# Expert weights read with eight neighbouring rows per partition, in a mixture-of-experts inference step

## What is computed

```python
logits = t @ w_router + b_router                # 320 x 32
top_v, top_i = lax.top_k(logits, 4)             # four experts per token
gates = jax.nn.softmax(top_v, axis=-1)
# for each expert, on the tokens that chose it:
uu  = xb @ w_up[eid] + b_up[eid]                # (n,1024) @ (1024,2048)
glu = jnp.minimum(uu[:, :1024], 7.0)
lin = jnp.clip(uu[:, 1024:], -7.0, 7.0)
act = glu * jax.nn.sigmoid(1.702 * glu) * (lin + 1.0)
yb  = act @ w_down[eid] + b_down[eid]           # (n,1024) @ (1024,1024)
```

## Time and profile before

| | |
|---|---|
| runs | 1298.5, 1301.34, 1304.66 us; median 1301.34 us |
| profiled execution, first to last instruction | 1299.7 us |
| TensorE busy | 1211.8 us, 93% |
| VectorE, ScalarE, GpSimd busy | 28%, 20%, 3% |
| read from HBM | 438 MB, 340 GB/s over the span |
| first up product to the end | 306.3 us to 1299.7 us |

### The profile page before, as it was taken

The page is one execution under the profiler, slowest core; times in us unless marked ns, Lnnn a source line. Parts: engine busy times, 40 slices in busy tenths (PEclk is TensorE's granted clock), DMA queues, the critical chain, the costliest instruction groups (busy, mean ns, idle before and its releaser), DMA issues.

```text
span 1299.7 us, 14599 instructions
## 1 busy us (share of the span) xinstructions
PE 1211.8 (93%) x5802; PEld 579.9 (45%) x5802; DVE 361.8 (28%) x668; ACT 259.9 (20%) x415; POOL 36.5 (3%) x90
## 2 busy tenths in 40 slices
PE   5999999998999999999999999999999999999995
PEld 4788789893333333333333333333333333333331
DVE  3545675622112222121212121222122121212123
ACT  5463352412111111111111111111111111111112
POOL 2002400000000000000000000000000000000000
PEclk9999999998889999999999999999999999999998
DMA  8550524479889999999999999999999999999861
GB/s 296 214 198 1 178 85 146 165 286 403 345 351 377 418 413 417 413 417 412 412 419 413 420 412 419 413 417 413 418 413 418 412 417 416 412 420 371 344 255 42
DMA packets 90801, 442.27 MB, mean 340 GB/s; under 512 B 3915, under 2 KB 16787, under 8 KB 57968
## 3 DMA queue, kind: packets, MB, share of 16 engines
q1 hardware_dynamic: 57952, 312.75, 59.8%
q10 hardware_dynamic: 31760, 125.85, 24.3%
q0 software_dynamic: 1056, 3.21, 0.7%
HBM read 438.06 MB, written 3.73 MB: 340 GB/s over the span
## 4 chain that ended last, share of the span: by engine, by line
PE 89%; DVE 4%; ACT 4%; issue 2%; ACTq 1%; POOL 0%; DVEq 0%; POOLq 0%
PE ps L441 35%; PE ps L455 17%; PE ps L331 14%; PE ps L462 7%; PE ps L418 7%; ACT regionP L588 2%; DVE regionP L724 2%; PE ps L433 1%; DVE regionP L688 1%; PE ps L1702 1%; PE ps L424 1%; ACTq L611 1%; PE ps L430 1%; ACT regionP L624 1%; PE ps L1487 1%
## 5 line engine op out<-in xcount | busy, mean ns | idle before, releaser
L441 PE MATMUL ps<-regionA,regionP 128*64 128x512 f32 x1024 | 224.9, 597 | 14.0 <-DVE regionP L688 14.0
L441 PE MATMUL ps<-regionB,regionP 128*64 128x512 f32 x1024 | 226.1, 600 | 0.0
L455 PE MATMUL ps<-regionD,regionP 128*64 128x512 f32 x992 | 218.2, 592 | 0.0
L667 DVE TENSOR_TENSOR regionP<-ps,regionP 128x512 f32<-128x512 f32 x32 | 22.1, 692 | 673.4 <-PE ps L448 673.4
L441 PEld LDWEIGHTS ps<-regionA,regionP 128*64 128x64 f32 x1024 | 74.4, 138 | 155.5 <-issue 152.4
L441 PEld LDWEIGHTS ps<-regionB,regionP 128*64 128x64 f32 x1024 | 72.7, 138 | 139.5 <-issue 139.2
L455 PEld LDWEIGHTS ps<-regionD,regionP 128*64 128x64 f32 x992 | 72.2, 137 | 140.7 <-issue 140.4
L604 ACT ACTIVATE regionP<-ps 128x1024 f32<-128x1024 f32 x32 | 32.7, 1023 | 458.3 <-PE ps L441 458.3
L462 PE MATMUL ps<-regionP 128*128 128x512 f32 (+1 forms) x192 | 94.0, 613 | 19.4 <-DVE regionP L724 13.2
L418 PE MATMUL ps<-regionP 128*64 128x512 f32 x384 | 92.0, 615 | 7.1 <-ACT regionP L588 4.8
L331 PE MATMUL ps<-roundedP,roundedA 128*128 128x320 f32 x272 | 85.3, 313 | 1.3 <-DVE regionP L1335 1.3
(11 more groups left out here) (276 smaller groups left out, 1034.1 us busy)
## 6 DMA issues: line engine op xcount, KB each, us to landing
regionA<-in_w_up SPq DMA_DIRECT2D x64, 2048.0 KB, 13.2
regionB<-in_w_up SPq DMA_DIRECT2D x64, 2048.0 KB, 10.7
regionD<-in_w_down ACTq DMA_DIRECT2D x60, 2048.0 KB, 18.0
regionA<-in_w_in SPq DMA_DIRECT2D x4, 2048.0 KB, 13.9
regionB<-in_w_mk SPq DMA_DIRECT2D x4, 1024.0 KB, 9.7
regionD<-in_w_mv SPq DMA_DIRECT2D x4, 1024.0 KB, 22.7
regionD<-in_w_out SPq DMA_DIRECT2D x4, 1024.0 KB, 12.5
regionD<-in_w_mq SPq DMA_DIRECT2D x4, 1024.0 KB, 5.0
```

What stands on the lines that cost most here:

```text
L441: ins = pe.matmul(ps[64 * half:64 * half + 64, n_, :], XTe[:, k % 4, k // 4, :], w[:, k, 1024 * half + 512 * n_:1024 * half + 512 * n_ + 512],
L455: ins = pe.matmul(ps[64 * n_:64 * n_ + 64, 6, :], lin[:, k, :], w[:, k, 512 * n_:512 * n_ + 512], start=(k == 0), stop=(k == KT - 1))
L667: dve.tensor_tensor(glu, u[:, :, 0:SLOTS], be[:, 0:8].unsqueeze(2).broadcast_to([P, KT, SLOTS]), ALU.add).then_inc(S("glu"), 1)
```

## The change

The contraction rows are dealt to the partitions in another way: partition p holds the eight neighbouring rows 8p to 8p+7, and block k is made of the rows 8p + k. A load of 2 MB then reads, for each partition, one piece of 16 KB (two rows of 8 KB, or four of 4 KB) at a distance of 64 KB (`w_up`) or 32 KB (`w_down`) from that of the next partition. Whatever meets the weights in a product is permuted to match: the tokens' columns (`Hm`), the gain (`g_rows`, loaded a second time in the new order), the up bias (`rows_of`) and the columns of `U`. The three reads that do the permuting step over eight elements (32 bytes) from one element to the next.

```diff
+        g_rows = small[:, 144:152]
@@ up_src, down_src, and the first loads in the SyncE block
-            return src.rearrange("a (k p) f -> p (a k) f", p=P)
+            return src.rearrange("a (p k) f -> p (a k) f", p=P)
@@ moe_act
+            def turned_rows(act):
+                return act.activation(U.rearrange("s (k p) -> s k p", k=KT),
+                                      ps[:, 0:2, :].rearrange("s b f -> s (b f)").rearrange("s (p k) -> s k p", k=KT), ACT.Copy)
...
-                act.activation(U[:, :], ps[:, 0:2, :].rearrange("p b f -> p (b f)"), ACT.Copy).then_inc(S("up_read"), 1)
+                turned_rows(act).then_inc(S("up_read"), 1)
@@ moe_dve
-                g = g_moe.rearrange("p (h q) -> p q h", h=2).unsqueeze(3).broadcast_to([P, 4, 2, SLOTS])
+                g = g_rows.rearrange("p (h q) -> p q h", h=2).unsqueeze(3).broadcast_to([P, 4, 2, SLOTS])
...
+            dve.wait_ge(S("g_rows_in"), 16)
             tokens().then_inc(S("tokens_in"), 1)
@@ GpSimd block
             pool.dma_start(buprow[0:E, :], a["b_up"][0]).then_inc(S("bup_in"), 16)
+            pool.dma_start(g_rows, a["norm_moe"][0].rearrange("(p k) -> p k", k=KT)).then_inc(S("g_rows_in"), 16)
@@ ScalarE block
-                act.activation(Hm[0:n, i, :], acc[0:n, i, :], ACT.Copy, scale=rs2[0:n, i:i + 1]).then_inc(S("Hm"), 1)
+                act.activation(Hm[0:n, i, :].rearrange("t (k p) -> t k p", k=KT), acc[0:n, i, :].rearrange("t (p k) -> t k p", k=KT),
+                               ACT.Copy, scale=rs2[0:n, i:i + 1]).then_inc(S("Hm"), 1)
@@ TensorE block
-            turn("bup", [(E * f, buprow[0:E, 128 * f:128 * f + 128], E, P) for f in range(16)])
+            rows_of = buprow[0:E, :].rearrange("e (h p k) -> e h k p", h=2, k=KT)
+            turn("bup", [(E * f, rows_of[:, f // KT, f % KT, :], E, P) for f in range(16)])
```

More of the change, by code:

```diff
@@ L810, in load_up0 @@
             def load_up0(i):
-                load(upA[:, 2 * i:2 * i + 2, :], a["w_up"][0, 0].rearrange("(k p) f -> p k f", p=P)[:, 2 * i:2 * i + 2, :], f"upA_in{i}")
+                load(upA[:, 2 * i:2 * i + 2, :], a["w_up"][0, 0].rearrange("(p k) f -> p k f", p=P)[:, 2 * i:2 * i + 2, :], f"upA_in{i}")
             has(sp, "oT3")
@@ L824, in _ @@
             for i in range(4):
-                load(upB[:, 2 * i:2 * i + 2, :], a["w_up"][0, 1].rearrange("(k p) f -> p k f", p=P)[:, 2 * i:2 * i + 2, :], f"upB_in{i}")
+                load(upB[:, 2 * i:2 * i + 2, :], a["w_up"][0, 1].rearrange("(p k) f -> p k f", p=P)[:, 2 * i:2 * i + 2, :], f"upB_in{i}")
             has(sp, "mo7")
@@ L829, in _ @@
             for i in range(2):
-                load(wdn[:, 4 * i:4 * i + 4, :], a["w_down"][0, 0].rearrange("(k p) f -> p k f", p=P)[:, 4 * i:4 * i + 4, :], f"down_in{i}")
+                load(wdn[:, 4 * i:4 * i + 4, :], a["w_down"][0, 0].rearrange("(p k) f -> p k f", p=P)[:, 4 * i:4 * i + 4, :], f"down_in{i}")
             moe_sync(sp)
```

## The result

The changed kernel takes 1305.55 us, the median of 20 runs (1299.85 to 1309.99), where the kernel before takes 1299.4 us on the same chip (20 runs, 1295.32 to 1305.0). The ratio over all runs is 1.0044, with a 95% interval of 1.0027 to 1.0061: about 5.7 us slower (the medians lie 6.2 us apart), within the 0.5% that was called no change, and twice to three times the 2.2 us of the forecast. The profiled execution took 1304.0 us. First its page: span, busy time by engine, and the DMA strip.

What follows compares the result with a forecast made beforehand. TensorE's order of work was taken to set the time, the DMA right behind; loop gain 0, prologue costs 0.35 + 0.6 + 0.7 + 0.55 = 2.2 us on the 1301.34 us median gave 1303 us, 8-in-10 range 1296 to 1311.

Steps and rivals of the forecast that it cites:

- What bounds the kernel: Steady expert loop: TensorE's order of work sets the time, 60.61 us per pair, with the DMA right behind it.
- the thin margin: Expert loop: the second half of w_down lands only 0.9 us before TensorE's down product needs it.
- The 16 KB pieces: Weight loads: 623 ns per piece, DMA share from 101.5% to 98.6%; hidden behind TensorE, so gain costed at 0.
- Rival A: Expert loop: the DMA falls behind and TensorE waits for w_down in every expert, 1316 to 1329 us; chance 0.10.
- The decisive piece of 641 ns: Weight loads: above this time per 16 KB piece, the DMA would ask for more per expert than before.
- The copy of U: ScalarE's stepped copy after the up product: hidden except for the first expert, 0 to 0.7 us, taken as 0.35.
- Hm: Three stepped ScalarE copies ahead of the first gather: 0 to 2.2 us, taken as 1.1, half given back, 0.6.
- The bias's turn: 16 TensorE instructions in the prologue with a stepped stationary operand: 0 to 1.5 us, taken as 0.7.
- the load of g_rows: GpSimd's extra load issue ahead of the iota in the prologue, covered by nothing: 0.55 us, between 0.50 and 0.96.
- The sum: Prologue costs together: 0.35 + 0.6 + 0.7 + 0.55 = 2.2 us, between 0.5 and 5.4 us.
- Rival B: Prologue: stepped reads at their upper ends, 5.4 us, plus one more slow-clock stretch, 2.6 us: 1309 us; chance 0.08.
- First up product at 307 to 310: Sign that the forecast is right: the first up product starts at 307 to 310 us instead of 306.3.

Runs made afterwards that it cites:

- the layout alone: Changed kernel with new weight layout and copy of U kept, but bias, Hm and gain as before and no g_rows load: 1301.26 us, ratio 1.0006.
- the reads alone: Changed kernel with its permuted reads and g_rows load kept, but the weights laid out as before: 1306.23 us, ratio 1.0057 to the kernel before.
- second mended version: Changed kernel with Hm read with the step from PSUM and g_rows loaded behind the iota, bias still turned: 1299.61 us, ratio 1.0013.
- first mended version: Changed kernel with Hm read from PSUM, g_rows loaded behind the iota, bias loaded permuted in 32-byte pieces and not turned: 1305.02 us, ratio 1.0048.

## Why the prediction was right, and where its sum was off

**What bounds the kernel: right.** The pair stayed at 60.6 us, no product of the steady part waits for weights, and the layout alone is at 1.0006. Half the up work taken away gave nothing before, so the DMA did stand right behind TensorE, as the thin margin said.

**The 16 KB pieces: right, in price and in worth.** Forecast 623 ns and 98.6%; measured 623 and 615 ns, 98.4%. Costed at 0; the runs gave -0.2 us. What the step missed is a second reason why `w_down`'s margin grows: its pieces are now as large as those of `w_up`, so that, with turns by piece and work in both queues, it gets half of the bytes where it got a third. Rival A (the DMA falls behind) did not happen. The decisive piece of 641 ns was not reached: pieces 32 or 64 KB apart cost nothing to be seen. The 3% that the Trainium skill ("DMA: Bandwidth & Descriptors", "Latency and other measured facts") reports for rows 512 KiB apart do not show at these distances: the changed kernel with half the up blocks moved 428 GB/s over 500 us, where the steady part before had 415.

**The copy of U: mis-sized, 0.35 forecast, 0 measured.** The page's row of the copies:

```profile
L579 ACT ACTIVATE regionP<-ps 128x1024 f32<-128x1024 f32 x32 | 32.8, 1024 | 453.7 <-PE ps L442 453.7
```

1024 ns against the 1.02 us of the earlier trace rows: ScalarE reads PSUM with the step as fast as without.

**Hm: the step that failed in size.** Forecast 1.1 us gross and 0.6 net, with an upper bound of 2.2. Its line in the profile after (ns, shortest, median, longest):

```profile
L1151 ACT ACTIVATE regionP<-regionP x3: 2115/2116/2126, 300.9 to 304.9; 128x1024 f32<-128x1024 f32 x2, 64x1024 f32<-64x1024 f32 x1
```

2.12 us for each where it was 1.1, so about +1.0 each and 2.9 in all: 0.95 ns per element, above the 0.72 that VectorE's write with a step had given as the far end. Some 1.8 us of it reach the end, as the runs without it show, so that 1.1 of 2.9 us are given back where the prediction had half. The reason that it gave fits the profile after: the slow stretch covers 3.10 us of the gather, which takes 4.34 us instead of 5.40. But the layout alone has 4.21 us without the step, so these profiles do not prove it. The rule of the Trainium skill ("SBUF — State Buffer", "SBUF: two separate sides") on two hits per line agrees with the trace for ScalarE's read of SBUF (1.9 times as long) and for the stationary operand (0.77 us in 16 products); its word on PSUM, which names matmuls, does not carry over to ScalarE's reads of PSUM, which lost nothing.

**The bias's turn and the load of g_rows: right.** Forecast 0.7 and 0.55; measured 0.77 and 0.60.

**The sum.** 1.8 + 0.77 + 0.60 = 3.2 us against 3.0 measured at equal clock; forecast 2.2, nearly all of the lack in Hm. The other 2.7 us are the term that the forecast did not have: more time at 1.2 GHz. With it the gap of 5.7 us lies above the sum's own upper end of 5.4. That the time still came within 2.5 us of 1303 is in part luck: the forecast stood on the median of three runs, 1301.34 us, and twenty runs have 1299.4. Rival B had it (one more stretch, 2.6 us), for a pause ahead of the gather. The profile after shows one more stretch elsewhere, at 44 to 54 us, and the kernel of before with half the up work, whose start is that of the kernel before, shows the low clock there too, in its chain of waits:

```profile
47.25 1.77 PE ps L1530 x6
```

So that stretch does not need the step, and the reads alone have the step without the stretch. Whether the lower mean clock follows from the delay or from where the work falls otherwise stays open. For the delay speaks that Hm's copies made twice gave a part of it, and that the second mended version, with Hm off the chain, has the clock of the kernel before; against it, that the first mended version, with the early start, lost as much in the loop. "First up product at 307 to 310" was wrong in this profile (313.75) for the same reason: 0.6 + 0.77 + about 2 for Hm make 3.4 of the 7.45 us; the rest is clock. Without a low clock there, the reads alone start it at 309.53.

## What to carry to other kernels

In this kernel two queues that shared full DMA engines divided them by piece size: give the load with the fewest buffers pieces at least as large as the others', and never enlarge the pieces of its rival alone. When a transfer is hidden behind an engine, a cheaper transfer buys nothing, and what is put on the chain for its sake is paid (here 3.0 us, and 2.7 more with the clock); put a read with a step where the data is still in PSUM, if ScalarE is to do it. Before a difference of a few us is explained from two profiles, set the runs of both against their granted clock.

## What the runs showed that was not expected

- Turns by piece: the same 8 MB of `w_up` per expert in pieces twice as large made the kernel with half the up work 138 us slower, or 68 us faster when `w_down`'s grew as well.
- The kernel before was balanced to the edge: with 220 us less for TensorE to do it took 1307.72 us. Only with `w_down` in pieces of 16 KB did a shorter TensorE order become time, 47 and 60 us.
- A step of 32 bytes took ScalarE from 1138 to 2116 ns for 1024 elements read from SBUF, and from 1023 to 1024 ns for as many from PSUM.
- An earlier start brought slow stretches into a loop that had none (0.50 at 604.70 us), and 3 us of chain that were saved did not show in the time.
